# Adding the last term to x1 where it already lies: accumulating transfers into the outputs

## The reference, cut to what matters

```python
def encoder_layer(x, c, p, l):
    ada = jax.nn.silu(c) @ p['w_ada'][l] + p['b_ada'][l]
    sh1, sc1, gt1, sh2, sc2, gt2 = jnp.split(ada[:, None, :], 6, axis=-1)
    h = rms_norm(x, p['norm_pre_mix'][l]) * (1 + sc1) + sh1
    x = x + gt1 * rms_norm(token_mixer(h, p, l), p['norm_post_mix'][l])
    h = rms_norm(x, p['norm_pre_ffn'][l]) * (1 + sc2) + sh2
    y = expert_choice_ffn(h, p['w_router'][l], p['w_gate_e'][l], p['w_up_e'][l], p['w_down_e'][l])
    return x + gt2 * rms_norm(y, p['norm_post_ffn'][l])
```

## Time and profile before

| what | us |
|---|---|
| median of 3 runs (lowest, highest) | 3752.38 (3751.66, 3755.83) |
| the profiled execution's own time | 3751.38 |
| its span in the trace | 3749.7 |
| TensorE busy | 3427.7 (91% of the span) |
| VectorE busy | 2186.2 (58%) |
| ScalarE busy | 1611.0 (43%) |
| GpSimd busy | 758.4 (20%) |

### The profile page before, as it was taken

One profiled execution on the slowest core, in us unless ns is written; L12 is line 12 of the kernel. 1 busy time (PEld: TensorE's weight loads), 2 busy tenths in 40 slices (PEclk: granted clock), 3 DMA queues, 4 the chain that ended last, 5 costly groups with the idle time before them and its releaser, 6 DMA issues. The chain is left out here.

```text
span 3749.7 us, 57954 instructions
## 1 busy us (share of the span) xinstructions
PE 3427.7 (91%) x21784; PEld 2891.1 (77%) x21784; DVE 2186.2 (58%) x3963; ACT 1611.0 (43%) x2478; POOL 758.4 (20%) x874
## 2 busy tenths in 40 slices
PE   6999999998999999799999559999999999999991
PEld 4777777676777777687777559999999999999990
DVE  3554455444688888554455565555555555555545
ACT  3665566453444444344444124444344444344442
POOL 1111101340234434222233101111111111111005
PEclk9999999998999999899999669999999999999995
DMA  6434344556555454565664435555555555555567
GB/s 216 160 122 148 132 142 144 168 178 186 174 155 158 144 160 141 172 199 193 204 219 169 168 105 183 168 171 164 162 169 166 163 173 162 162 171 164 162 216 283
DMA packets 540147, 637.26 MB, mean 170 GB/s; under 512 B 82528, under 2 KB 420544, under 8 KB 539712
## 3 DMA queue, kind: packets, MB, share of 16 engines
q1 hardware_dynamic: 490032, 481.58, 40.3%
q0 software_dynamic: 44800, 148.96, 12.3%
q10 hardware_dynamic: 5136, 4.31, 0.3%
HBM read 507.86 MB, written 126.91 MB: 169 GB/s over the span
## 5 line engine op out<-in xcount | busy, mean ns | idle before, releaser
L2679 DVE TENSOR_TENSOR moe_w_lo<-c_w_raw,moe_w_hi 128x2048 fp32r<-128x2048 f32 x192 | 439.8, 2290 | 371.4 <-ACT moe_w_hi L2627 371.4
L110 PE MATMUL moe_pg<-moe_x_hi,moe_w_hi 128*128 128x320 f32 x2048 | 635.1, 310 | 1.4 <-DVE moe_x_lo L2717 1.4
L111 PE MATMUL moe_pg<-moe_x_lo,moe_w_hi 128*128 128x320 f32 x2048 | 633.4, 309 | 0.0
L112 PE MATMUL moe_pg<-moe_x_hi,moe_w_lo 128*128 128x320 f32 x2048 | 633.3, 309 | 0.0
L2627 ACT CAST moe_w_hi<-c_w_raw 128x2048 fp32r<-128x2048 f32 x192 | 364.1, 1896 | 152.3 <-PE moe_pd L2835 77.0
L110 PEld LDWEIGHTS moe_pg<-moe_x_hi,moe_w_hi 128*128 128x128 f32 x2048 | 385.0, 188 | 2.4 <-issue 1.5
L111 PEld LDWEIGHTS moe_pg<-moe_x_lo,moe_w_hi 128*128 128x128 f32 x2048 | 385.0, 188 | 0.6
L112 PEld LDWEIGHTS moe_pg<-moe_x_hi,moe_w_lo 128*128 128x128 f32 x2048 | 385.0, 188 | 0.0
L110 PE MATMUL gla_pd<-gla_h_hi,gla_w_hi 128*128 128x512 f32 x640 | 262.2, 410 | 26.4 <-DVE gla_h_lo L1228 24.3
L111 PE MATMUL gla_pd<-gla_h_lo,gla_w_hi 128*128 128x512 f32 x640 | 252.8, 395 | 0.0
L112 PE MATMUL gla_pd<-gla_h_hi,gla_w_lo 128*128 128x512 f32 x640 | 252.6, 395 | 0.0
(11 more groups left out here) (367 smaller groups left out, 7549.9 us busy)
## 6 DMA issues: line engine op xcount, KB each, us to landing
c_w_raw<-in_w_gate_e_dram SPq DMA_DIRECT2D x64, 1024.0 KB, 5.0
c_w_raw<-in_w_up_e_dram SPq DMA_DIRECT2D x64, 1024.0 KB, 5.0
c_w_raw<-in_w_down_e_dram SPq DMA_DIRECT2D x64, 1024.0 KB, 4.9
c_w_raw<-in_w_in_dram SPq DMA_DIRECT2D x80, 512.0 KB, 3.8
c_w_raw<-in_w_in_dram SPq DMA_DIRECT2D x35, 1024.0 KB
scratch_gate<-gla_sg POOLq DMA_DIRECT2D x80, 256.0 KB, 2.4
mix_sg<-scratch_gate SPq DMA_DIRECT2D x40, 512.0 KB, 4.6
c_h_raw<-scratch_hT SPq DMA_DIRECT2D x37, 512.0 KB, 6.7
```

Of the source, the lines that this page charges most:

```text
L110: pe.matmul(out, w_hi, x_hi, start=start, stop=False)
L111: pe.matmul(out, w_hi, x_lo, start=False, stop=False)
L112: return pe.matmul(out, w_lo, x_hi, start=False, stop=stop)
L2679: dve.tensor_tensor(w_lo[:, m % 2], w_raw[:, m % 2], w_hi[:, m % 2].bitcast(F32), ALU.subtract).then_inc(s_wlo, 1)
```

## The change

The scratch tensor `x1` goes. The mixer stores the tiles of `x1` straight into the output tensors (a new helper, `out_rows`, picks the rows). The last expert and the last phase load no `x1`. In `phase_final` VectorE only multiplies `y` by its root and the gate, and GpSimd, in place of the store, issues a transfer that adds the tile to the rows already in the output (`accum_op=ALU.add`). Before the first tile GpSimd waits for the mixer's stores. There are ten buffers each for `y` and `o`, and the load of `y` now waits for VectorE's result of nine tiles ago.

```diff
-def phase_mix(nc, K, I, S):
+def out_rows(outs, t):
+
+    n = N_PROMPT // P
+    return outs[0][0, t * P:(t + 1) * P, :] if t < n else outs[1][0, (t - n) * P:(t - n + 1) * P, :]
+
+
+def phase_mix(nc, K, I, S, outs):
...
-                    sp.dma_start(S["x1"][n * P:(n + 1) * P, :], mix[:, t]).then_inc(s_last, 16)
+                    sp.dma_start(out_rows(outs, n), mix[:, t]).then_inc(s_last, 16)
...
-                        pool.dma_start(S["x1"][n * P:(n + 1) * P, :], mix[:, t]).then_inc(s_x1st, 16)
+                        pool.dma_start(out_rows(outs, n), mix[:, t]).then_inc(s_x1st, 16)
...
-                        if is_exp(e, N_EXP - 1) and m == 0:
-                            sp.wait_ge(K.x1_stored, 16 * TPB * (NB - 1))
-                            sp.wait_ge(K.last_stored, 16 * TPB)
-                        if is_exp(e, N_EXP - 1) and m < N_KEPT:
-                            sp.dma_start(K.x1[:, m], S["x1"][m * P:(m + 1) * P, :]).then_inc(K.s_x1, 16)
...
-    NY, NO = 6, 4
+    NY, NO = 10, 10
...
                 for t in range(NT):
-                    wait(sp, s_m, t - NY + 1)
+                    wait(sp, s_o, t - NY + 1)
                     sp.dma_start(y[:, t % NY], S["y"][t * P:(t + 1) * P, :]).then_inc(s_y[t % NY], 16)
...
-                    if t < NT - N_KEPT:
-                        n = N_KEPT + t
-                        act.dma_start(x1[:, t], S["x1"][n * P:(n + 1) * P, :]).then_inc(s_x, 16)
...
-            def store(pool, t):
-                n = N_PROMPT // P
-                dst = outs[0][0, t * P:(t + 1) * P, :] if t < n else outs[1][0, (t - n) * P:(t - n + 1) * P, :]
-                pool.wait_ge(s_o, t + 1)
-                pool.dma_start(dst, o[:, t % NO]).then_inc(s_st[t % NO], 16)
...
+                def add(t):
+                    pool.wait_ge(s_o, t + 1)
+                    pool.dma_start(out_rows(outs, t), o[:, t % NO], accum_op=ALU.add).then_inc(s_st[t % NO], 16)
+
+                pool.wait_ge(K.x1_stored, 16 * TPB * (NB - 1))
+                pool.wait_ge(K.last_stored, 16 * TPB)
                 for t in range(NT):
...
                     if t >= 2:
-                        store(pool, t - 2)
-                store(pool, NT - 2)
-                store(pool, NT - 1)
+                        add(t - 2)
+                add(NT - 2)
+                add(NT - 1)
...
-                                             in1=K.gate1[:, 0 if t < N_PROMPT // P else 1], op0=ALU.mult, op1=ALU.mult).then_inc(s_m, 1)
-                    dve.wait_ge(s_m, t + 1)
-                    if t < N_KEPT:
-                        kept = K.x1[:, t]
-                    else:
-                        dve.wait_ge(s_x, 16 * (NT - N_KEPT))
-                        kept = x1[:, t - N_KEPT]
-                    dve.tensor_tensor(o[:, t % NO], o[:, t % NO], kept, ALU.add).then_inc(s_o, 1)
+                                             in1=K.gate1[:, 0 if t < N_PROMPT // P else 1], op0=ALU.mult, op1=ALU.mult).then_inc(s_o, 1)
```

More of the change, by code:

```diff
@@ L2489, in phase_route @@
         done(K, M)
-N_KEPT = 12
 def final_memory(nc, K):
-    K.x1 = K.sb("x1", [P, N_KEPT, D])
-    K.s_x1 = K.sem("x1_kept")
     K.s_gate2 = K.sem("gate2_kept")
@@ L2849, in phase_final @@
 def phase_final(nc, K, I, S, outs):
-    NY, NO = 6, 4
+    NY, NO = 10, 10
     with Mem(nc, "fin") as M:
-        y, x1, o = M.sb("y", [P, NY, D]), M.sb("x1", [P, NT - N_KEPT, D]), M.sb("o", [P, NO, D])
-        junk = M.sb("junk", [P, NO, D], BF16)
+        y, o = M.sb("y", [P, NY, D]), M.sb("o", [P, NO, D])
+        junk = M.sb("junk", [P, 4, D], BF16)
         ss, r = M.sb("ss", [P, NT]), M.sb("r", [P, NT])
-        s_st = [M.sem(f"stored{i}") for i in range(NO)]
-        s_q, s_v, s_r, s_m, s_o = M.sem("squares"), M.sem("mean"), M.sem("rstd"), M.sem("normed"), M.sem("made")
-        s_y, s_x = [M.sem(f"y_loaded{i}") for i in range(NY)], M.sem("x1_loaded")
+        s_st = [K.sem(f"added{i}") for i in range(NO)]
+        s_q, s_v, s_r, s_o = M.sem("squares"), M.sem("mean"), M.sem("rstd"), M.sem("made")
+        s_y = [M.sem(f"y_loaded{i}") for i in range(NY)]
         with nc.Block() as block:
@@ L2868, in _ @@
                 for t in range(NT):
-                    if t < NT - N_KEPT:
-                        n = N_KEPT + t
-                        act.dma_start(x1[:, t], S["x1"][n * P:(n + 1) * P, :]).then_inc(s_x, 16)
                     act.wait_ge(s_y[t % NY], 16 * (t // NY + 1))
-                    wait(act, s_q, t - NO + 1)
-                    act.activation(junk[:, t % NO], y[:, t % NY], ACT.Square, accum_out=ss[:, t:t + 1]).then_inc(s_q, 1)
-            def store(pool, t):
-                n = N_PROMPT // P
-                dst = outs[0][0, t * P:(t + 1) * P, :] if t < n else outs[1][0, (t - n) * P:(t - n + 1) * P, :]
-                pool.wait_ge(s_o, t + 1)
-                pool.dma_start(dst, o[:, t % NO]).then_inc(s_st[t % NO], 16)
+                    wait(act, s_q, t - 3)
+                    act.activation(junk[:, t % 4], y[:, t % NY], ACT.Square, accum_out=ss[:, t:t + 1]).then_inc(s_q, 1)
             @block.gpsimd
             def _(pool):
+                def add(t):
[3 more added lines that the diff above has]
+                pool.wait_ge(K.last_stored, 16 * TPB)
                 for t in range(NT):
@@ L2898, in _ @@
                 dve.wait_ge(K.s_gate2, 16)
-                dve.wait_ge(K.s_x1, 16 * N_KEPT)
                 for t in range(NT):
@@ L2925, in encoder_layer @@
         ("gate", [2 * KD, P, T]),
-        ("x1", [T, D]), ("xn", [T, D]), ("y", [T, D]))}
+        ("xn", [T, D]), ("y", [T, D]))}
     with Mem(nc, "c") as K:
@@ L2932, in encoder_layer @@
         routing_memory(nc, K)
-        phase_mix(nc, K, I, S)
+        phase_mix(nc, K, I, S, outs)
         phase_route(nc, K, I, S)
```

## The result

| | before | after |
|---|---|---|
| median of 12 executions of each, us | 3752.57 | 3764.43 |
| profiled execution, us | 3751.38 | 3765.13 |
| its span, us | 3749.7 | 3763.3 |
| first load of `y` issued, us | 3680.03 | 3681.84 |
| last stage: from there to the end of the span, us | 69.7 | 81.5 |

The changed kernel is slower: the ratio is 1.0030, with a 95% interval of 1.0022 to 1.0037. The medians differ by 11.9 us; 9.7 had been forecast, and 3764.43 stands beside the 3762.1 of the forecast. One of the 12 executions before took 3970.58 us, far off all the others: it counts in the median and not in the ratio.

The account below looks back on a forecast made before the run. The last stage was taken as 52 us transfer-bound, then 13 us VectorE-bound; afterwards transfers bind. Adding costs 25.2 us, loads return 10.0 and VectorE 5.6: 9.7 us later in the span, forecast 3762.1 us, range 3754 to 3770.

Parts of the forecast that it names:

- main term: Last stage: 20 adds at 209 GB/s take the DMA engines 50.2 us, 25.2 us more than plain stores.
- the price: Last stage: an add moves 209 GB/s, read from scatters with add, twice the engine time of a store.
- The part that comes back: Last stage: eight x1 loads gone return 10.0 us, VectorE's twenty additions gone return 5.6 us.
- The 5.6 us: Last stage before: this much was VectorE's, not the transfers', and comes back if transfers no longer wait.
- the tail: Last 13 us of the stage before, from 3734: bound by VectorE, 1.28 + 1.22 us a tile without a gap.
- rival B: Last stage: GpSimd's mean, power and add issue set the pace, 3.94 us a tile, kernel 3777.5 us; chance 0.12.
- The costs put at nothing: Mixer's stores moved to outputs: 0; last expert's twelve loads removed: gain 0, at most 1 us; buffer waits: no hold-up.
- A: Last stage: an add costs little more than a store, kernel not slower, 3747.0 us or 3743; chance 0.15.
- The low limit of main memory: Last stage: main memory binds at about 358 GB/s, crossings take 87.9 us, kernel 3774.8 us; chance 0.02.

Follow-up runs that it names:

- e1: Changed kernel with a plain store in place of each add, x1 left out of the outputs: 3736.71 us, ratio 0.9956 to before, last stage 56.1 us.
- e3: Kernel before with only x1 kept in the outputs, stored there by the mixer and loaded from there: 3751.85 us, ratio 1.0001, last stage 69.7 us.
- e4: Changed kernel with the buffers of before, six for y and four for o: 3764.93 us, ratio 1.0035 to before, last stage 81.8 us.
- e5: Kernel before with deeper buffers alone, eight for y and ten for o: 3752.81 us, ratio 1.0004, last stage 71.4 us.
- e9: Kernel before with eight y and ten o buffers and the last stage's stores issued by SyncE: 3750.38 us, ratio 0.9998, last stage 68.9 us.
- e12: As e9, but GpSimd makes two tiles' roots in one mean and one power from the third tile: 3748.25 us, ratio 0.9992, stage 65.2 us.
- e2: Changed kernel with adds in every second tile only, the others stored plainly without x1: 3750.83 us, ratio 0.9995 to before, last stage 69.0 us.
- e8: Changed kernel with three more one-column GpSimd operations for each tile, results unused: 3772.48 us, ratio 1.0054 to before, last stage 90.3 us.
- e10: As e9, but the first eight tiles added by transfer, the other twelve kept from the last expert: 3746.61 us, ratio 0.9987, stage 66.3 us.
- e6: Kernel before with deeper buffers, twelve x1 tiles kept from the last expert, the last eight added by transfer: 3754.05 us, ratio 0.9999, stage 72.2 us.

## Why the prediction was right, and where it was off

**The sign and the main term.** 20 adds in place of 20 stores were put at 25.2 us more and measured at 25.4. The row chosen for the price, 209 GB/s from the indirect scatters of before, was the right one: direct adds alone moved 210 to 211.

**The part that comes back.** Loads gone and VectorE's additions gone were put at 10.0 + 5.6 us. Between the kernel before and e1, which differ in that and in the moved stores and buffers that cost nothing (e3, e4), the stage fell by 13.6. This is the 2 us by which the forecast was short (81.5 in place of 79.4 for the stage), and it isn't the adds' doing: without them the same sum gives 1.5 + 49.9 + 2.7 = 54.1 us, and e1 took 56.1. Some 0.9 us of it lies at the start: from 3684 to 3690 only 357 GB/s moved, after the change and in e1 alike, where the sum had 420 from 1.5 us behind the first load. The rest was not taken apart. Nor were the two terms, 10.0 and 5.6, ever removed one at a time; the runs show their sum.

**The 5.6 us: the tail was read rightly, and what stood beside it was missed.** The tail of the kernel before is VectorE's own 2.46 us a tile, as the prediction says. What it lacks is the lockstep with GpSimd, which takes over where the waits for stores are gone: e5 shows that deeper buffers alone return nothing, and e9 and e12 that with deep buffers the lockstep sets the pace. The forecast for the changed kernel was spared this, because there VectorE has no addition left that could hold a power; all 20 powers take 0.55 to 0.58 us. That was in part luck: rival B's text says that VectorE would be busy for less of a tile, but not why this should shorten a power. The sign that I passed over stood in the earlier trace rows: a power that takes 547 ns at least and 1534 in the middle is an operation that something holds up. I used those rows to argue against rival B and did not ask what made the spread.

**The costs put at nothing.** The moved stores (e3), the loads out of the last expert (86.00 of 86 us busy on either side), and the waits for buffers (e4) each cost nothing that can be measured, as argued.

**The rivals.** A fell with e1 and e2. One reason given against it was misread: in the stretch of the earlier trace rows with 209 GB/s only scatters moved, and no weight load beside them. B did not happen, as argued, and its mechanism is real: pushed past its point in e8, it set the end. By B's own sum with e8's numbers (first add at 3693.6, 19 x 3.71 us, then 5.3 and 2.2) the span ends at 3771.6, and it ended at 3771.2; parts of it cancel, since the last three adds were issued together from 3756.8 on and took up to 11.1 us to land. The low limit of main memory, with a chance of 0.02, isn't there: adds alone moved 210 to 211 GB/s, and each byte of the output is read and written, which makes 420 to 422 across main memory. The Trainium skill (DMA: Bandwidth & Descriptors, section "Where 436 GB/s comes from") has main memory bind at about 358 GB/s for a core; these 420 do not agree with it, and the measurement decides. Whether the 420 are set by the engines or by main memory at a higher limit no run here separates, since plain traffic and adds reach the same 420 of crossings.

## What to carry to other kernels

A transfer that accumulates saves a load and a vector operation but takes the DMA engines about twice the time of a store, so it costs where they are the bound; that it pays where they have slack follows from this, but no run here shows it. Eight adds put first (e10) gave a stage of 66.3 us, put last (e6) one of 72.2. Not all of the 5.9 us is the order: in e10 SyncE also issues the stores, and between e5 and e9 that went with 2.5 us. When a short operation shows a minimum far below its median, find out beside what it runs before using either number. Undo one part at a time: the same 12 us could have been put down to buffers, to moved stores or to GpSimd. e4 took the buffers back, e3 made the move alone, and e8 slowed GpSimd until its pace did set the end.

## What the runs showed of the hardware that I had not expected

**GpSimd waits out VectorE's operations.** A power of 128 x 1 takes 0.55 us while VectorE is idle and 1.53 to 1.55 when it starts just behind the start of an addition; it then ends about 0.4 us behind that addition. A mean takes 0.18 us alone, and 1.28 when it starts with a product, ending 0.05 us behind it. The operations added in e8 show it again: the first of the three starts with the product and takes 1.28 us, and the next two, behind its end, take 0.19 each. The wait doesn't depend on GpSimd's work: the mean does next to nothing and still takes the whole of VectorE's operation. The Trainium skill (SBUF — State Buffer, section "Who interferes with whom") says that a VectorE operation with two inputs in the on-chip memory and a GpSimd operation that reads that memory exclude each other, and that the later one is blocked until the first is done; both of VectorE's operations here have two such inputs, and the ends in e5 and e9 agree with it to 0.06 us for the mean. The further 0.4 us belong to the power and not to the addition: a power that starts with a product ends 0.43 us behind it (before, 3708.97 to 3710.63 against 3710.20), and a mean that meets an addition ends 0.06 behind it (e12, 3719.12 against 3719.06). What they consist of, no run here shows.

**A direct add is issued in 0.89 us, a store in 0.60** (medians of the changed kernel and of e1). The prediction had bounded it between 0.60 and 1.58.
